# Two SwiGLU layers of a two-block model: seven half-size products in place of eight

## What is computed

```python
def swiglu(h, wg, wu, wd):
    return (jax.nn.silu(h @ wg) * (h @ wu)) @ wd

for i in range(2):
    sh1, sc1, g1, sh2, sc2, g2 = split(silu(c) @ ada_w[i] + ada_b[i])
    x = x + g1 * mix_i(rms_norm(x, norm_mix_g[i]) * (1 + sc1) + sh1)   # i = 1: a convolution block
    h = rms_norm(x, norm_ffn_g[i]) * (1 + sc2) + sh2
    x = x + g2 * swiglu(h, ffn_w_gate[i], ffn_w_up[i], ffn_w_down[i])
return rms_norm(x, final_norm_g)
```

## Time and profile before

| | |
|---|---|
| median of 2 runs | 1542.34 us (1540.51 to 1544.16) |
| the profiled execution | 1544.05 us, span 1542.4 us |
| TensorE busy | 1447.2 us, 94% of the span |
| VectorE busy | 631.4 us, 41% |
| ScalarE busy | 253.0 us, 16% |
| GpSimd busy | 226.4 us, 15% |
| granted TensorE clock, mean | 0.973 |
| dense layer 0, first matmul to last | about 934 to 1164 us |
| dense layer 1 | about 1306 to 1533 us |

### The profile page before, as it was taken

How to read it: one execution, slowest core, us unless ns; L and a number is a source line. 1 busy time by engine, 2 the same in 40 slices (tenths; PEclk the granted TensorE clock), 3 DMA queues, 4 the chain that set the end, 5 groups by cost and what they waited for, 6 DMA issues and landing times. The chain is left out here.

```text
span 1542.4 us, 18568 instructions
## 1 busy us (share of the span) xinstructions
PE 1447.2 (94%) x7579; PEld 1079.9 (70%) x7579; DVE 631.4 (41%) x1132; ACT 253.0 (16%) x543; POOL 226.4 (15%) x305
## 2 busy tenths in 40 slices
PE   6999998967678999999999999999999999999997
PEld 2877646534335888778888887777767878877774
DVE  3488857312124677835451102333307982000002
ACT  3121211000002112213352001000002352000001
POOL 5081100000002001533445004000001000000000
PEclk9999999988789899999999999999999999999999
DMA  9977667999998688747664448988543403444440
GB/s 349 323 258 262 236 248 325 390 415 418 418 413 275 207 296 288 260 127 187 137 161 140 140 140 297 355 306 302 179 137 110 164 1 110 137 163 150 149 136 27
DMA packets 173052, 352.33 MB, mean 228 GB/s; under 512 B 6921, under 2 KB 134080, under 8 KB 155568
## 3 DMA queue, kind: packets, MB, share of 16 engines
q1 hardware_dynamic: 163840, 310.73, 56.0%
q0 software_dynamic: 9136, 40.55, 8.8%
HBM read 350.09 MB, written 1.16 MB: 228 GB/s over the span
## 5 line engine op out<-in xcount | busy, mean ns | idle before, releaser
L2529 PE MATMUL PS<-HT,ring 128*128 128x256 f32 x1616 | 352.5, 379 | 0.0
L2529 PEld LDWEIGHTS PS<-HT,ring 128*128 128x128 f32 x1616 | 307.0, 190 | 49.4 <-issue 8.6
L1769 PE MATMUL PS<-HT,ring 128*128 128x256 f32 x1152 | 261.4, 385 | 0.1
L1769 PEld LDWEIGHTS PS<-HT,ring 128*128 128x128 f32 x1152 | 217.6, 192 | 38.1 <-issue 9.1
L2838 DVE TENSOR_TENSOR hid<-PS,silu 128x512 f32<-128x512 f32 x22 | 15.2, 692 | 357.5 <-PE PS L2529 357.5
L2545 PE MATMUL PS<-ring,hid 128*128 128x512 f32 x320 | 140.6, 592 | 0.0
L2545 PEld LDWEIGHTS PS<-ring,hid 128*128 128x128 f32 x320 | 60.8, 190 | 68.0 <-issue 67.0
L1257 PE MATMUL PS<-ring_extra,slot_rows 128*32 128x256 f32 x592 | 61.6, 462 | 26.0 <-DMA ring_extra<-in_expert_w_gate 16.4
L1944 PE MATMUL PS<-ring,y_T 128*128 128x256 f32 x384 | 83.3, 379 | 0.0
L1944 PEld LDWEIGHTS PS<-ring,y_T 128*128 128x128 f32 x384 | 72.9, 190 | 9.9
L2723 ACT ACTIVATE silu<-PS 128x512 f32<-128x512 f32 x22 | 13.1, 597 | 392.4 <-PE PS L2529 392.4
(11 more groups left out here) (557 smaller groups left out, 1767.9 us busy)
## 6 DMA issues: line engine op xcount, KB each, us to landing
ring<-in_hy_w_in SPq DMA_DIRECT2D x40, 1024.0 KB, 7.8
ring_extra<-in_w_ada SPq DMA_DIRECT2D x24, 1024.0 KB, 8.5
ada_stage<-in_ada_w POOLq DMA_DIRECT2D x24, 1024.0 KB, 7.9
ring<-in_ffn_w_gate SPq DMA_DIRECT2D x22, 1024.0 KB, 5.3
ring<-in_ffn_w_up SPq DMA_DIRECT2D x22, 1024.0 KB, 5.3
ring<-in_ffn_w_down SPq DMA_DIRECT2D x22, 1024.0 KB, 4.8
ring_extra<-in_expert_w_gate SPq DMA_DIRECT2D x20, 1024.0 KB, 18.9
ring_extra<-in_expert_w_down SPq DMA_DIRECT2D x18, 1024.0 KB, 25.7
```

Of the source, the lines that this page charges most:

```text
L1769: mm = pe.matmul(dst, w[:, k, half * P:(half + 1) * P], HT[:, k, :], start=(k == 0), stop=(k == KT - 1))
L2529: mm = pe.matmul(dst, w[:, k, m * P:(m + 1) * P], HT[:, k, :], start=(k == 0), stop=(k == KT - 1))
```

## The change

In chunks 1 to 9 of both layers (`CHUNKS_7`) gate and up together are treated as one product of two-by-two blocks: tokens in two halves against two halves of the width, and the two halves of the width against gate and up. In place of eight block products there are seven (`product`, P1 to P7, each 4 matmuls of 256 columns), with sums of blocks before and after (the form of Strassen's method with few sums). The slices of `HT`, or sums of them in `hsum`, are now the stationary side, and the weights, or sums of them in `wsum`, the moving one, so that the results have tokens on the partitions.

- Sums of tokens: `sum_rows_of_x`, four VectorE operations of 512 columns, once a layer.
- Sums of weights, for each chunk ahead of it: four operations of 1024 columns, one of them in place in the up tile. In layer 0 VectorE makes them (`sum_weights`), in layer 1 GpSimd does, in a new loop at the end of its program, and VectorE waits for it in `sum_weights`.
- Combining: VectorE makes the sums of P1 to P7 in eleven operations of 256 columns a chunk, two of which are the products with silu; ScalarE takes silu in two halves.
- Each chunk's rows are turned back by four transposes of 128 x 128 on TensorE in the chunk after (`turn_hid`), and ScalarE moves them to `hid` (`move_hid`). The down product is as before, in two halves with P7 between them.
- P1 to P7 and the transposes take half a bank each in banks 0 to 3, one place apiece for all chunks, so a product waits until the one of the chunk before has been read.
- Chunks 0 and 10 keep the old form. The loops over pairs of chunks are written out on TensorE, ScalarE and VectorE.
- `stage` has three slots in place of six; `wsum` takes the rest. The 24 modulation adds are spread over chunks 1 to 9, three in each of the first six and two in the others.

The diff, cut to its core:

```diff
-    stage = carve(stage_conv, 0, [6, 2 * D])
+    stage = carve(stage_conv, 0, [3, 2 * D])
+    wsum = carve(stage_conv, 6 * D, [2, 3, 4, CW])
+    P1, P2, P5, P3, P6, P4, P7, TURN = (PS[:, b // 2, b % 2 * CW:(b % 2 + 1) * CW] for b in range(8))
 # TensorE
+            def turn_hid(f, e, m):
+                if m == 0:
+                    pe.wait_ge(hid_ready, FFN_CHUNKS * f + e + 1)
+                    pe.wait_ge(combined, row_sum(f, e, 4))
+                else:
+                    pe.wait_ge(silu_ready, ACT_MARKS[f, e + 1, ("move", 0)])
+                for i in range(TT):
+                    mm = pe.transpose(TURN[:, i * P:(i + 1) * P], hid_rows[:, e % 2, i, m * P:(m + 1) * P], ident[:])
+                mm.then_inc(sevens, 1)
+            def seven(f, e):
+                arrive(pe, n_g)
+                arrive(pe, n_u)
+                pe.wait_ge(combined, weights_summed(f, e))
+                if e > 1:
+                    pe.wait_ge(combined, row_sum(f, e - 1, 2))
+                product(P2, rows(1, 0), half(gate, 1))
+                product(P1, rows(0, 0), half(gate, 0)).then_inc(used, 1)
+                if e > 1:
+                    pe.wait_ge(combined, row_sum(f, e - 1, 5))
+                product(P5, hs7(0), ws7(0))
+                if e > 1:
+                    turn_hid(f, e - 1, 0)
+                product(P3, hs7(3), half(up, 1))
+                if e > 1:
+                    turn_hid(f, e - 1, 1)
+                    pe.wait_ge(combined, row_sum(f, e - 1, 6))
+                else:
+                    wait_hid(f, 0, 0)
+                product(P6, hs7(1), ws7(1)).then_inc(sevens, 1)
+                arrive(pe, n_d)
+                wait_hid(f, e - 1, 0)
...
+                down_part(n_d, (e - 1) % 2, 0, e == 1)
+                wait_hid(f, e - 1, 1)
+                product(P7, hs7(2), half(up, 0)).then_inc(used, 1)
+                down_part(n_d, (e - 1) % 2, 1, e == 1).then_inc(used, 1)
+                pe.wait_ge(combined, row_sum(f, e, 2))
+                product(P4, rows(1, 1), ws7(2)).then_inc(sevens, 1)
 # ScalarE
+                for e in CHUNKS_7:
+                    act.wait_ge(combined, row_sum(f, e, 0))
+                    act.activation(gate_act[:, e % 2, 0], gate_pre[:, 0], ACT.Silu).then_inc(silu_ready, 1)
+                    if e > 1:
+                        move_hid(e - 1)
+                    act.wait_ge(combined, row_sum(f, e, 6))
+                    act.activation(gate_act[:, e % 2, 1], gate_pre[:, 1], ACT.Silu).then_inc(silu_ready, 1)
 # VectorE
+            def sum_weights(f, e):
+                if f == 1:
+                    dve.wait_ge(biased_x, TT + e)
+                    dve.sem_inc(combined, 1)
+                    return
...
+                step(dve.tensor_tensor(t1, up[:, 0:4, :], gate[:, 0:4, :], ALU.subtract))
+                step(dve.tensor_tensor(t2, up[:, 4:8, :], t1, ALU.subtract))
+                step(dve.tensor_tensor(up[:, 0:4, :], up[:, 4:8, :], up[:, 0:4, :], ALU.subtract))
+                dve.tensor_tensor(t4, gate[:, 4:8, :], t2, ALU.subtract).then_inc(combined, 1)
+            def seven(f, e, adds):
...
+                n = 1 if len(adds) > 2 * (LAST_E - e) else 0
+                dve.wait_ge(used, chunk(f, "g", e) + 1)
+                step(dve.tensor_copy(gate_pre[:, 0], P2))
+                dve.tensor_tensor(gate_pre[:, 0], P1, gate_pre[:, 0], ALU.add).then_inc(combined, 1)
...
+                    sum_weights(f, e + 1)
...
+                some(n)
+                dve.wait_ge(sevens, PE_MARKS[f, e, "P6"])
+                step(dve.tensor_copy(up_pre[:, 0], P1))
+                dve.tensor_tensor(up_pre[:, 0], P6, up_pre[:, 0], ALU.add).then_inc(combined, 1)
...
+                step(dve.tensor_tensor(up_pre[:, 1], P5, up_pre[:, 0], ALU.add))
+                dve.tensor_tensor(up_pre[:, 1], P3, up_pre[:, 1], ALU.add).then_inc(combined, 1)
...
+                step(dve.tensor_tensor(hid_rows[:, e % 2, 0], up_pre[:, 1], gate_act[:, e % 2, 0], ALU.mult))
+                some(min(1, len(adds)))
+                dve.wait_ge(used, chunk(f, "u", e) + 1)
+                dve.tensor_tensor(up_pre[:, 0], P7, up_pre[:, 0], ALU.add).then_inc(combined, 1)
...
+                dve.tensor_tensor(up_pre[:, 2], P5, up_pre[:, 0], ALU.add).then_inc(combined, 1)
+                some(min(1, len(adds)))
+                dve.wait_ge(sevens, PE_MARKS[f, e, "P4"])
+                dve.tensor_tensor(gate_pre[:, 1], P4, up_pre[:, 0], ALU.add).then_inc(combined, 1)
...
+                dve.tensor_tensor(hid_rows[:, e % 2, 1], up_pre[:, 2], gate_act[:, e % 2, 1], ALU.mult).then_inc(hid_ready, 1)
 # GpSimd
+            for e in CHUNKS_7:
+                if e > 1:
+                    pool.wait_ge(used, chunk(1, "g", e - 1) + 1)
+                else:
+                    pool.wait_ge(used, B_PW2 + 4)
...
+                step(pool.tensor_tensor(t1, up[:, 0:4, :], gate[:, 0:4, :], ALU.subtract))
+                step(pool.tensor_tensor(t2, up[:, 4:8, :], t1, ALU.subtract))
+                step(pool.tensor_tensor(up[:, 0:4, :], up[:, 4:8, :], up[:, 0:4, :], ALU.subtract))
+                pool.tensor_tensor(t4, gate[:, 4:8, :], t2, ALU.subtract).then_inc(biased_x, 1)
```

More of the change, by code:

```diff
@@ L2530, in half_rows, with down_part @@
                 return mm
[L2532 to L2540, removed]
-                w = w_slot(n, D)
[L2542 to L2547, removed]
+            def down_part(n, par, f, first=False):
+                w = w_slot(n, D)
+                for i, h in pieces():
+                    mm = pe.matmul(PS[:, 4 + 2 * i + h, :], hid[:, par, f, i * P:(i + 1) * P],
+                                   w[:, f, h * 512:(h + 1) * 512], start=first and f == 0, stop=False)
+                return mm
             def last_down(f, n, par):
@@ L2564, in turn_vectors @@
                 mm.then_inc(made, 1)
-            def ffn(f, norm, early=None, late=None):
[L2567 to L2577, removed]
-                    else:
[L2579 to L2604, removed]
@@ new lines, in product @@
+            def product(dst, lhs, rhs):
+                for k in range(KT // 2):
+                    mm = pe.matmul(dst, lhs[k], rhs[k], start=(k == 0), stop=(k == KT // 2 - 1))
+                return mm
+            def turn_hid(f, e, m):
[7 more added lines that the diff above has]
+                mm.then_inc(sevens, 1)
@@ L2720, in ffn, with whole_silu, move_hid @@
             def ffn(f):
[L2721 to L2723 removed]
+                def whole_silu(e, bank):
+                    act.wait_ge(used, chunk(f, "g", e) + 1)
+                    act.activation(silu[:, e % 2], PS[:, bank, :].rearrange("p (a b) -> p a b", a=2), ACT.Silu)\
                         .then_inc(silu_ready, 1)
[L2725 to L2731, removed]
+                def move_hid(e):
+                    for m in range(2):
+                        act.wait_ge(sevens, PE_MARKS[f, e + 1, ("turn", m)])
+                        act.activation(hid[:, e % 2, m], TURN, ACT.Copy).then_inc(silu_ready, 1)
+                whole_silu(0, 2)
+                for e in CHUNKS_7:
[5 more added lines that the diff above has]
+                    act.activation(gate_act[:, e % 2, 1], gate_pre[:, 1], ACT.Silu).then_inc(silu_ready, 1)
+                whole_silu(LAST_E, 0)
+                move_hid(LAST_E - 1)
             root(0, 0)
@@ L2823, in turn @@
                                       ALU.add).then_inc(left, 1)
[L2825 to L2838, removed]
+            def add(n):
+                i, j = n // 6, n % 6
+                dve.wait_ge(arrived[j], 16 * (i + 1))
+                if n >= 3:
+                    dve.wait_ge(ada_summed, n - 2)
+                dve.scalar_tensor_tensor(out=acc[:, j % 3, :], in0=stage[:, j % 3, :],
+                                         scalar=cv[:, 2 * i + j // 3:2 * i + j // 3 + 1], in1=acc[:, j % 3, :],
+                                         op0=ALU.mult, op1=ALU.add).then_inc(ada_summed, 1)
@@ new lines, in sum_rows_of_x @@
+            def sum_rows_of_x(norm):
+                dve.wait_ge(left, 4 * (norm + 1))
+                dve.wait_ge(right, 4 * (norm + 1))
+                a11, a12, a21, a22 = (HT[:, 4 * h:4 * h + 4, i * P:(i + 1) * P] for i in range(TT) for h in range(2))
+                step(dve.tensor_tensor(hsum[:, 0], a21, a22, ALU.add))
+                step(dve.tensor_tensor(hsum[:, 2], a11, a21, ALU.subtract))
+                step(dve.tensor_tensor(hsum[:, 1], hsum[:, 0], a11, ALU.subtract))
+                step(dve.tensor_tensor(hsum[:, 3], a12, hsum[:, 1], ALU.subtract))
@@ L2979, in _ @@
             f = 1
[L2980 to L2983, removed]
-            for e in range(2 + 2 * PAIRS, FFN_CHUNKS):
-                one(f, e % 2, up_done(f, e), e + 1)
+            sum_rows_of_x(2)
+            sum_weights(f, 1)
+            whole_hid(f, 0, 3)
+            for e in CHUNKS_7:
+                seven(f, e, [])
+            whole_hid(f, LAST_E, 1)
```

123 lines of the change are left out of this document (105 added, 18 removed).

## The result

| | before | after |
|---|---|---|
| median of 2 runs | 1542.34 us | 1522.62 us (1521.93 to 1523.32) |
| ratio, 95% interval | | 0.9874 (0.9843 to 0.9905) |
| span of the profiled execution | 1542.4 us | 1520.3 us |
| one middle chunk of either dense layer | 20.68 us | 19.40 us |
| norm ahead of layer 1, see below | 11.20 us | 18.17 us |

The kernel is 1.3% faster, 19.7 us in the medians where 16 were forecast. VectorE has 126 us more to do, GpSimd 86 more, TensorE 27 less, and the end is still set by TensorE. L2585 are the products P1 to P7, L2562 the down matmuls of these chunks, L2556 gate and up in the chunks that keep the old form, L2595 the transposes.

A forecast was written before the change was run, and what follows sets the result against it. TensorE was taken to bound the kernel, with nothing else in the dense layers. 1544.05 us profiled, less 19.6 over 18 chunks, plus 3 in layer 1's norm, gave 1527.5, or 1526 for the median; range 1518 to 1540.

The forecast's parts named there:

- Matmuls removed: TensorE, 18 chunks of both dense layers: 28 matmuls of 256 columns for 32, 1.73 us less a chunk.
- Transposes: TensorE, same chunks: four added at 0.11 us each plus 0.2 for exposed weight loads, 0.64 us a chunk.
- Waits met: Dense chunks: TensorE's added waits are met when it arrives and cost nothing.
- VectorE in layer 0: First six chunks, three modulation adds each: 17.3 us of work in 19.6, hidden, 3.1 us to spare before the transpose.
- GpSimd in layer 1: Four weight sums of 2.36 us a chunk, done at 13.4 us; P6's sum at 14.5, 3.4 us to spare.
- rival 1: Layer 1, wait ahead of P6's copy: GpSimd's sums set the pace, kernel slower, 1574 us at 4.7 a sum; chance 0.08.
- Norm ahead of layer 1: VectorE's small operations and row scalings wait beside GpSimd's first sums: 0 to 6 us lost, 3 taken.
- my worst case: Norm ahead of layer 1: small ops and both scalings wait, second scaling ends near 1309.1 instead of 1303.2, 6 us.
- Transfers: Up tiles and modulation slabs with fewer slots: 0 to 9 us over nine chunks, taken as 0.

The follow-up runs named there:

- with the clock held up: Changed kernel with 19 matmuls on the identity in place of 5 ahead of layer 1's norm: median 1518.31 us, ratio 0.9872.
- without the waiting: Changed kernel with GpSimd's first sums of layer 1 waiting for both row scalings, not pw2's last matmul: median 1517.63 us, ratio 0.9852.
- the kernel run again: The changed kernel as it is, nothing altered: median 1522.89 us against 1540.51 of the kernel before, ratio 0.9887.
- the best versions measured for both layers: Changed kernel with layer 1's weight sums on VectorE, none on GpSimd: 1515.03 us; with GpSimd's first sums there after both row scalings: 1517.63 us.

## Why the prediction was right, and where its terms were off

The mechanism was right: inside the dense layers TensorE sets the time, the change takes four matmuls out of a chunk, and the new chains on VectorE and GpSimd fit inside it. The forecast of 1526 us was 3.4 above the median. Term by term:

- *Matmuls removed*, 1.73 us a chunk: as said. P2 with P1, 8 matmuls, take 3.45 us, 0.431 each.
- *Transposes*, 0.64 us a chunk forecast, 0.44 measured. The 0.2 for weight loads left exposed behind the two pairs isn't there; the run with four a pair shows 0.11 each and no more. This term alone is 18 x 0.2 = 3.6 us, the chunk was 19.40 and not 19.59.
- *Waits met*: yes. TensorE has no gap in the windows of either layer.
- *VectorE in layer 0*: forecast 3.1 us of reserve, read 3.6. That this is a true bound is shown by the run with 5 us more a chunk, which cost 15.0 us.
- *GpSimd in layer 1*: sums forecast done 13.4 us into a chunk, measured 13.3 (1328.37 to 1341.71); 3.4 us of reserve forecast, 3.3 read. One operation more is free and two are not, as rival 1's place and price said. Rival 1 itself did not occur: 2.35 us an operation, as in the earlier trace rows.
- *Norm ahead of layer 1*: forecast 3 us with 6 as the worst case, measured 7.0. This was the step most off. The waiting alone is 6.0 us (15.90 with the clock held up, 9.87 without the waiting), twice what I took and as much as my worst case. It is more than the scalings and small operations: an addition with two SBUF inputs waits as well, 1.5 us. The rest is TensorE's clock, at nothing in the sum: it costs 2.3 us in the changed kernel and cost 1.3 in the same norm before (11.20 against 9.87), 1.0 more. The Trainium skill, GPSIMD Engine Reference, section 8. Key points, names VectorE instructions with two SBUF inputs next to the two-port modes; I weighed that and left it out of the sum because no row showed it. The trace agrees with the page: 0.69 us became 2.22, and an addition of that size with one input in PSUM kept its 0.69.
- *Transfers*: costed at nothing, and no VectorE wait for one stands in the dense windows.

The two misses, 3.6 us too little gained and 4 too little lost, all but cancel, and that is luck. With the measured terms the sum would be 1542.34 - 23.0 + 7.0 = 1526.3, the forecast over again, and the measured median lies 3.7 under it. These 3.7 us, 1.6 by the medians of the kernel run again, stand in no term of the prediction and stay open; ahead of the dense layers four profiles of the kernel before alone differ by 7.7 us.

Without the loss in that norm come the best versions measured for both layers, at 1515.03 and 1517.63 us.

## What to carry to other kernels

Before moving elementwise work to an idle GpSimd, look at what VectorE does while it runs, not at how idle either is: here the sums were free in the chunks, where VectorE stood waiting, and cost 7 us in one norm, by a start that one wait put 3 us too early. Work that is hidden behind TensorE has a reserve which can be read off the trace as the time between its result and its use; up to it additions are free, beyond it every chunk pays the excess. A gain by fewer matmuls is worth the intervals between their starts, and a small transpose costs its interval too, here 0.11 us where its record says 0.27.

## What the runs showed of the hardware

- Beside a GpSimd sum of two SBUF inputs some VectorE operations wait until that sum ends. An addition with two SBUF inputs did (0.69 us became 2.22) and so did TENSOR_SCALAR operations that read SBUF, one of two elements a partition (0.17 became 1.06 and 1.28) as well as two of 1024 columns (1.41 became 5.23). An addition with one input in PSUM (L3099, 0.69), a reduction (L3105, 0.16) and a reciprocal (L2891, 0.17) beside the same sums kept their time.
- The GpSimd sum that starts while such a held-up VectorE operation is still running takes some 0.33 us more (2.67 and 2.68 in place of 2.35); the one that starts after it doesn't (L3177, 2.34).
- Back-to-back float32 transposes of 128 x 128 cost TensorE 0.11 us each between products: two delay the next product by 0.22 us, four by 0.44.
- The same norm with the same operations, and no GpSimd sum beside it that holds them up, took 9.86 us with the granted clock at 1.00 and 11.20 to 11.24 where it was 0.52 during the transposes of the profile shown.
